# Passes over the experts taken in pairs, with seven places for loaded units and three for split ones in place of five and four

## The chip, the cores and the metric

The kernel runs on one core of one Trainium2 chip. The metric is device time in microseconds (us) of that core. The kernel before has a median of 1789.32 us over 3 runs (1788.54 to 1793.39). The execution that was profiled took 1784.65 us, of which 1782.8 us is the span of its instructions.

## The reference

Two layers of a block with attention, a gated linear recurrence and a feed-forward part, in float32. Only the feed-forward part of the second layer, a mixture of experts on 256 tokens, bears on the change:

```python
def swiglu(h, w1, w3, w2):
    return (jax.nn.silu(h @ w1) * (h @ w3)) @ w2

def moe_ffn(h, router, w1, w3, w2):
    logits = (ht @ router).astype(jnp.float32)
    top_v, top_i = lax.top_k(logits, TOP_K)              # TOP_K = 2 of 8 experts
    wts = jax.nn.softmax(top_v, axis=-1)
    combine = jnp.sum(jax.nn.one_hot(top_i, N_EXPERTS) * wts[..., None], axis=1)
    # for each expert: acc + combine[:, e] * swiglu(ht, w1[e], w3[e], w2[e])
```

The model width is 1024 and the inner width of an expert 2816, so an expert has 3 x 1024 x 2816 weights, 34.6 MB, and all eight 277 MB. The 256 tokens choose two experts each, 512 choices in all, so some experts get many tokens and some few.

## The kernel before

Each expert is one pass. Its weights are cut into 33 units of 1 MB (128 x 2048 floats): for each of 11 chunks of 256 inner columns (FC = 11) two "up" units (w1 and w3, half of the model width each) and one "down" unit (w2). The experts are put in order of their token counts by the kernel itself (`places_ranked`, `columns_ordered`, `experts_ordered`, `ranked` and three times `next_task`, small operations of VectorE (DVE) spread over the first seven chunks of pass 0).

There are two kinds of pass. A full pass (0 to 4) has 128 places for tokens. It computes float32 products from three products of shorter floats (fp32r): ScalarE (ACT) copies a loaded unit `raw` to `w_hi` (`high(s)`), DVE subtracts to get `w_lo` (`low(s)`), and TensorE (PE) does 12 matmuls with each unit (`three`). A narrow pass (5 to 7, the experts with the fewest tokens) has 64 places and reads `raw` directly as float32, without a split, in matmuls that use half of the array's columns each (`up_narrow`, `down_narrow`). Pass 1, `WIDE`, is a full pass with 32 more places.

A pass is a pipeline of steps. In step i PE does the up units of chunk i (`up_chunk`), turns the products of chunk i-1 (`turn_chunk`, transposes) and does the down unit of chunk i-2 (`down_chunk`). ACT takes the silu of the up result (`silu`), DVE multiplies (`product`), and both copy what PE has turned (`columns_turned`, L1463 and L2104 for full, L1460 for narrow). Towards the end of a pass (chunk 7) the tokens of the next pass are picked by matmuls with a selection (`gather`, L2783); in the chunks 3 to 6 of the next pass the output of the last one goes back to its tokens (`scatter`, L2841, 4 pieces, each followed by an addition of DVE, `added`, L2084).

What sets the order:

- SyncE (SP) loads the units in the order in which PE uses them, into a ring of RAW_RING = 5 places. The place of a full unit is free once DVE has split it, that of a narrow unit once PE has used it.
- `w_hi` and `w_lo` have W_RING = 4 places. The split of unit s is written in ACT's and DVE's programs behind PE's use of unit s-4: after unit s-4 is used, ACT copies unit s, then DVE subtracts.
- Each engine runs its program in order and waits on semaphores: a late wait on ACT holds back everything written behind it.
- After the last chunk of pass 7 each engine decides by a branch whether an expert had more tokens than places (it reads `task_i`). For this input it hasn't, and the branch goes over the code of three spare passes to `finish`: ACT copies the last output (`ey_plain`, L1433), PE scatters it, DVE adds, and norm, gate and store follow. RAW_RING units of a spare expert are loaded before that is known, and SP waits for their arrival before it stores.

Of the kernel before, what the change touches and what calls it, by code (L numbers as in the profile page):

```python
# [32 lines left out]
P = 128  # L33
# [19 lines left out]
RING = 3  # L53
# [247 lines left out]
def run_steps(passes):  # L301

    g0, g1 = passes[0] * FC, (passes[-1] + 1) * FC
    for g in range(g0, g1 + 2):
        yield g if g < g1 else None, g - 1 if g0 <= g - 1 < g1 else None, g - 2 if g0 <= g - 2 else None


def pass_units():

    out = []  # L310
    for passes in RUNS:
        for up, _, down in run_steps(passes):
            out += [("up", up, 0), ("up", up, 1)] if up is not None else []
            out += [("down", down)] if down is not None else []
    assert len(out) == PASSES_OF * EXPERT_UNITS
    return out
# [6 lines left out]


def run_last(r):
    return (RUNS[r][-1] + 1) * FC - 1
# [12 lines left out]
NARROW, SLOTS = range(5, EXPERTS), 64  # L339
HALF_GROUPS = P // SLOTS  # L340


def is_narrow(p):

    return p in NARROW
# [11 lines left out]

SPLIT_LIST = [m for m, key in enumerate(UNIT_LIST) if not is_narrow(unit_of_expert(key)[0])]
SPLIT_OF = {m: s for s, m in enumerate(SPLIT_LIST)}

# [6 lines left out]
def split_limit(r):  # L367

    return split_end(r) + (0 if is_narrow(RUNS[r][-1]) else W_RING - 1)
# [8 lines left out]
LATE_SPLIT = SPLIT_OF[UNIT_AT["down", NARROW[0] * FC - 1]]  # L378
# [195 lines left out]
TURN_BANK, SCATTER_BANK = 2, 3  # L574
# [3 lines left out]
def build(nc, ctx, units, x_in, ctx_in, const_in, cols_in, wsm_in, gw2_in, lam_in, rope_in, out):  # L578
# [86 lines left out]
    picked = at("picked", A_GL + 2952, [P, 2, 3, EXPERTS])  # L665
    order, order_parts = at("order", A_AM + 320, [P, EXPERTS, EXPERTS]), at("order_parts", A_GL + 3888, [P, 3, EXPERTS, EXPERTS])
    xt_plain = at("xt_plain", A_ACTT, [P, 2, KT, P])
    selT_plain = at("selT_plain", A_GL + 1280, [P, 2, 2, P])
    eT_plain = at("eT_plain", A_GL + 1792, [P, 2, 256])
    ey_plain = at("ey_plain", A_OD, [P, 512])  # L670
# [13 lines left out]
    raw_more = [at(f"raw_more{i}", (A_V, A_GV)[i], [P, UNIT]) for i in range(2)]  # L684
    w_hi_more, w_lo_more = at("w_hi_more", A_X, [P, UNIT], F32R), at("w_lo_more", A_GG, [P, UNIT], F32R)
# [105 lines left out]
    hi_places = [w_hi[:, (first_w + i) % RING, :] for i in range(RING)] + [w_hi_more[:, :]]  # L791
    lo_places = [w_lo[:, (first_w + i) % RING, :] for i in range(RING)] + [w_lo_more[:, :]]
# [11 lines left out]
    def down_bank(p, h):  # L804

        return 4 + 2 * (p % 2) + h

    def up_bank(g):

        return 0 if g // FC == WIDE else (g + WIDE * FC) % 2  # L810

    def gather_bank(p, n):

        return SCATTER_BANK if p == WIDE + 1 else down_bank(p, n)
# [5 lines left out]
    def select_place(p):  # L820
        return sel if p < EXPERTS else sel_more[p - EXPERTS]
# [14 lines left out]
    def _(sp):  # L836
# [48 lines left out]
        load_more(RING + 1, lambda p: EXPERTS - p)  # L885
        ordered = {0: EXPERTS}
# [36 lines left out]
    def _(pool):  # L923
# [18 lines left out]
        def select_narrow(p):  # L942

            twice = const[:, C_IOTA:C_IOTA + SLOTS].unsqueeze(1).to_broadcast([P, HALF_GROUPS, SLOTS])
            for tt in range(2):
                pool.tensor_scalar(sel[:, tt, :].rearrange("p (j n) -> p j n", j=HALF_GROUPS), twice, route[:, tt, 4, p:p + 1],
                                   route[:, tt, 3, p:p + 1], ALU.is_equal, ALU.mult).then_inc(esem("sel"), 1)
# [11 lines left out]
        for p in range(1, EXPERTS):  # L959

            pool.wait_ge(esem("selT"), p)
# [15 lines left out]
    def _(act):  # L977
# [407 lines left out]
        def half_high(p, n):  # L1385
            act.wait_ge(esem("gathered"), 2 * p + n + 1)
            if is_narrow(p):
                act.activation(xt_plain[:, p % 2, 4 * n:4 * n + 4, 0:SLOTS],
                               psum[:, gather_bank(p, n), 0:4 * SLOTS].rearrange("p (k n) -> p k n", n=SLOTS),
                               ACT.Copy).then_inc(esem("xt_hi"), 1)  # L1390
                return
            act.activation(xt_hi[:, p % 2, 4 * n:4 * n + 4, :],
                           psum[:, gather_bank(p, n), :].rearrange("p (k n) -> p k n", n=P),
                           ACT.Copy).then_inc(esem("xt_hi"), 1)

        def selection_turned(p):
            act.wait_ge(esem("selT"), p + 1)
            if p >= 2:
                act.wait_ge(esem("scattered"), 4 * (p - 1))
            turned_into = selT_plain if is_narrow(p) else selT  # L1400
            act.activation(turned_into[:, p % 2, :, :], psum[:, SCATTER_BANK, 0:256].rearrange("p (t n) -> p t n", t=2),
# [24 lines left out]
        def output(p):  # L1426

            if p:
                act.wait_ge(esem("scattered"), 4 * p)
# [13 lines left out]
        def silu(g):  # L1443
# [5 lines left out]
            if g >= 2:  # L1449
                act.wait_ge(esem("act"), g - 1)  # L1450
            n = P if is_narrow(g // FC) else 256
            act.activation(e_sil[:, g % 2, 0:n], psum[:, up_bank(g), 0:n], ACT.Silu).then_inc(esem("sil"), 1)  # L1452

        def columns_turned(g):

            act.wait_ge(esem("turned"), g + 1)
            if g >= 2:
                wait_used(act, ("down", g - 2))
# [1675 lines left out]
```

## Time and profile before

| | |
|---|---|
| median of 3 runs | 1789.32 us |
| profiled execution | 1784.65 us, span 1782.8 us |
| PE, DVE, ACT busy | 94%, 57%, 44% of the span |
| HBM read | 404.73 MB, mean 229 GB/s over the span |
| full passes 2 to 4 | from 1212.3 us to 1515.3 us |
| narrow passes 5 to 7 | from 1515.3 us to 1766.1 us |
| matmul line L2273 (`three`) | 60% of the chain that ended last |

A time in the profile is from the span's start. The chain of waits follows the work that ended last back through what released it, so in a stretch where its pieces are all PE, PE sets the pace, and where a DMA stands between matmuls, the loads do. The busy share of PE overstates what it does, since a matmul is pipelined: in a full pass one stands for 0.39 us and the next begins 0.227 us after it. So times between starts are used below.

### The profile page before, as it was taken

How to read it: one execution, taken by the hardware profiler on the slowest of the kernel's cores; microseconds unless marked ns; L12 is line 12 of the kernel's file. 1: busy time of each engine (PE TensorE's matmuls, PEld its weight loads, DVE VectorE, ACT ScalarE, POOL GpSimd, SP SyncE). 2: the span in 40 equal slices, each digit the busy share in tenths (PEclk: the TensorE clock that was granted, in tenths of full speed). 3: DMA queues.
4: the chain of work that ended last, by engine and by line, in shares of the span. 5: the costliest groups of instructions: out<-in, count | busy, mean ns of one | idle time of the engine just before them, and what ended most of it. 6: DMA issues, size and time to landing. Idle time of an engine off the chain costs nothing.

```text
span 1782.8 us, 25642 instructions
## 1 busy us (share of the span) xinstructions
PE 1676.5 (94%) x10193; PEld 1294.4 (73%) x10193; DVE 1021.3 (57%) x1415; ACT 792.6 (44%) x1225; POOL 55.0 (3%) x40
## 2 busy tenths in 40 slices
PE   5999987999999999999977999999999999988896
PEld 3877656988888888797767887677788888544443
DVE  3326656677677533733676987657889897100012
ACT  4417544532212222734655766556677776100101
POOL 0000000000000000000000530000000000000000
PEclk9999968999999999999988999999999999999998
DMA  8411053154467532131013986668989998999998
GB/s 335 161 62 72 1 188 144 72 189 174 157 228 262 197 116 95 57 142 63 33 50 142 352 331 227 247 230 328 361 341 356 345 368 313 378 406 421 419 420 363
DMA packets 56831, 407.53 MB, mean 229 GB/s; under 512 B 6322, under 2 KB 6450, under 8 KB 7808
## 3 DMA queue, kind: packets, MB, share of 16 engines
q1 hardware_dynamic: 56128, 404.38, 59.2%
q8 instruction: 84, 1.38, 0.3%
q0 software_dynamic: 288, 0.79, 0.1%
q10 hardware_dynamic: 288, 0.63, 0.1%
q14 instruction: 43, 0.35, 0.1%
HBM read 404.73 MB, written 1.05 MB: 228 GB/s over the span
## 4 chain that ended last, share of the span: by engine, by line
PE 82%; DMA 7%; DVE 6%; ACT 4%; issue 1%; SPq 0%; POOL 0%; ACTq 0%; DVEq 0%
PE psum L2273 60%; DMA raw<-units 5%; PE psum L2887 4%; PE psum L2897 2%; PE psum L2783 2%; DMA raw_more<-units 2%; PE psum L2841 1%; PE psum L2913 1%; PE psum L2925 1%; PE psum L2290 1%; PE psum L2472 1%; PE psum L2299 1%; DVE w_lo L1572 1%; PE psum L2496 1%; ACT xn L1026 1%
## 5 line engine op out<-in xcount | busy, mean ns | idle before, releaser
L1572 DVE TENSOR_TENSOR w_lo<-raw,w_hi 128x1024 fp32r<-128x1024 f32 x130 | 153.0, 1219 | 143.9 <-ACT w_hi L990 143.5
L2273 PE MATMUL psum<-act_hi,w_hi 128*128 128x512 f32 (+1 forms) x608 | 220.3, 362 | 2.8 <-DVE w_lo L1572 2.8
L2273 PE MATMUL psum<-act_hi,w_lo 128*128 128x512 f32 (+1 forms) x608 | 218.1, 359 | 0.0
L2273 PE MATMUL psum<-act_lo,w_hi 128*128 128x512 f32 (+1 forms) x608 | 218.0, 359 | 0.0
L990 ACT ACTIVATE w_hi<-raw 128x1024 fp32r<-128x1024 f32 x130 | 130.4, 1053 | 164.2 <-DMA raw<-units 89.8
L2044 DVE TENSOR_TENSOR w_lo<-raw,w_hi 128x2048 fp32r<-128x2048 f32 x75 | 171.4, 2289 | 45.4 <-ACT w_hi L1378 45.1
L1378 ACT ACTIVATE w_hi<-raw 128x2048 fp32r<-128x2048 f32 x75 | 143.8, 1918 | 73.0 <-PE psum L2273 43.8
L2273 PE MATMUL psum<-w_hi,act_hi 128*128 128x256 f32 (+1 forms) x368 | 131.2, 357 | 4.3 <-DVE act_lo L1651 2.4
L2044 DVE TENSOR_TENSOR w_lo<-raw_more,w_hi 128x2048 fp32r<-128x2048 f32 x49 | 112.1, 2289 | 35.7 <-ACT w_hi L1378 35.4
L2273 PE MATMUL psum<-w_hi,xt_hi 128*128 128x512 f32 x332 | 132.2, 398 | 0.0
L2093 DVE TENSOR_TENSOR e_act<-e_sil,psum 128x256 f32<-128x256 f32 (+1 forms) x88 | 32.2, 366 | 172.6 <-ACT e_sil L1452 172.6
L2273 PE MATMUL psum<-w_lo,xt_hi 128*128 128x512 f32 x332 | 129.9, 391 | 0.0
L2273 PE MATMUL psum<-w_hi,xt_lo 128*128 128x512 f32 x332 | 129.7, 391 | 0.0
L2273 PEld LDWEIGHTS psum<-act_hi,w_hi 128*128 128x128 f32 x608 | 114.9, 189 | 19.6 <-DVE w_lo L1572 3.3
L2273 PEld LDWEIGHTS psum<-act_hi,w_lo 128*128 128x128 f32 x608 | 114.9, 189 | 17.4
L2273 PEld LDWEIGHTS psum<-act_lo,w_hi 128*128 128x128 f32 x608 | 115.0, 189 | 16.3
L2273 PE MATMUL psum<-w_lo,act_hi 128*128 128x256 f32 (+1 forms) x368 | 123.8, 336 | 0.0
L2273 PE MATMUL psum<-w_hi,act_lo 128*128 128x256 f32 (+1 forms) x368 | 123.5, 336 | 0.0
L1452 ACT ACTIVATE e_sil<-psum 128x256 f32<-128x256 f32 (+1 forms) x88 | 29.4, 334 | 198.3 <-PE psum L2887 194.4
L1378 ACT ACTIVATE w_hi<-raw_more 128x2048 fp32r<-128x2048 f32 x49 | 94.0, 1918 | 52.4 <-PE psum L2273 30.7
L1629 DVE SCALAR_TENSOR_TENSOR folded<-raw,c_cols,folded 128x512 f32<-128x512 f32 x140 | 101.5, 750 | 3.3
L2273 PEld LDWEIGHTS psum<-w_hi,act_hi 128*128 128x128 f32 x368 | 70.3, 191 | 27.5 <-issue 12.0
(364 smaller groups left out, 3210.5 us busy)
## 6 DMA issues: line engine op xcount, KB each, us to landing
raw<-units SPq DMA_DIRECT2D x275, 1024.0 KB, 5.1
raw_more<-units SPq DMA_DIRECT2D x107, 1024.0 KB, 6.8
X<-ctx_in SPq DMA_DIRECT2D x1, 1024.0 KB, 8.8
X<-x_in SPq DMA_DIRECT2D x1, 1024.0 KB, 10.8
out<-X SPq DMA_DIRECT2D x2, 512.0 KB, 3.0
const<-const_in ACTq DMA_DIRECT2D x1, 524.0 KB, 7.7
rope<-rope_in POOLq DMA_DIRECT2D x2, 256.0 KB, 4.8
wsm<-wsm_in SPq DMA_DIRECT2D x1, 384.0 KB, 7.8
```

The lines of the kernel that those rows point to most:

```text
L990: act.activation(w_hi[:, w_slot(i), part], raw[:, i % RING, part], ACT.Copy).then_inc(hi_ready, 1)
L1026: act.activation(junk(t), src(t), ACT.Square, accum_out=ssq[:, t:t + 1]).then_inc(done, 1)
L1378: act.activation(w_place(m)[0], raw_place(m), ACT.Copy).then_inc(esem("w_high"), 1)
L1452: act.activation(e_sil[:, g % 2, 0:n], psum[:, up_bank(g), 0:n], ACT.Silu).then_inc(esem("sil"), 1)
L1572: ins = dve.tensor_tensor(w_lo[:, w_slot(i), part], raw[:, i % RING, part], w_hi[:, w_slot(i), part].bitcast(F32), ALU.subtract)
L1629: ins = dve.scalar_tensor_tensor(total, part, share, total, ALU.mult, ALU.add)
L2044: dve.tensor_tensor(lo, raw_place(m), hi.bitcast(F32), ALU.subtract).then_inc(esem("w_ready"), 1)
L2093: dve.tensor_tensor(e_act[:, g % 2, 0:n], e_sil[:, g % 2, 0:n], psum[:, up_bank(g), n:2 * n], ALU.mult).then_inc(esem("act"), 1)
L2273: ins = pe.matmul(dst, lhs(a), rhs(b), start=first and n == 0, stop=last and n == 2)
L2783: ins = pe.matmul(psum[:, gather_bank(p, n), (k % 4) * slots:(k % 4 + 1) * slots], src[:, tt, k * P:(k + 1) * P], select_place(p)[:, tt, 0 ...
L2887: ins = pe.matmul(psum[SLOTS * j:SLOTS * (j + 1), up_bank(g), 0:2 * P].rearrange("p (g n) -> p g n", g=2), xt_plain[:, p % 2, k, 0:SLOTS], ...
L2897: ins = pe.matmul(psum[SLOTS * h:SLOTS * (h + 1), down_bank(p, 0), :], eT_plain[:, g % 2, SLOTS * j:SLOTS * (j + 1)], weight[:, j * D_MODE ...
```

## The change

Passes 2 to 7 are taken in pairs, a full and a narrow one side by side: (2,3), (4,5), (6,7). The narrow passes are now 3, 5 and 7, and a table `PLACE_OF_RANK` gives them the same three experts with the fewest tokens that 5, 6 and 7 had. In a step of a pair PE does the two up units of the full chunk, the two of the narrow one, turns both chunks of the step before, and does the full and then the narrow down unit. The loads follow the same order.

Passes 0 and 1 stay single. There the split of unit s is now written behind the use of unit s-3. In the pairs the split of a unit is written in its own step. The two places that `w_hi_more` and `w_lo_more` had become places for loaded units: RAW_RING = 7, W_RING = 3. A narrow pass has its own small buffers (`e_sil_plain`, `e_act_plain`, `sel_plain`), so that it can go beside a full one. The gather for the next pair is cut into pieces in the chunks 7 to 10, the scatters of the pair before stand in the chunks 2 to 9. The ranking in pass 0 has eight more tiny writes (`place_wanted`), two more comparisons and one more operation in each `next_task`. At the end two passes, 6 and 7, are still to be scattered.

```diff
+PLACE_OF_RANK = (0, 1, 2, 5, 3, 6, 4, 7)
-RAW_RING, W_RING = 5, 4
+RAW_RING, W_RING = 7, 3
+NARROW, SLOTS = (3, 5, 7), 64
+FIRST_PAIR = 2
+def run_steps(r):
+    rows = []
+    for p in RUNS[r]:
+        if not is_narrow(p):
+            beside = (p + 1,) if is_narrow(p + 1) else ()
+            rows += [tuple(q * FC + c for q in (p,) + beside) for c in range(FC)]
+    for i in range(len(rows) + 2):
+        yield tuple(rows[j] if 0 <= j < len(rows) else () for j in (i, i - 1, i - 2))
-def split_behind(r, key):
-    s = SPLIT_OF[UNIT_AT[key]] + W_RING
-    return [s] if s < split_limit(r) and s != LATE_SPLIT else []
+def splits_at(r, key):
+    s = SPLIT_OF[UNIT_AT[key]]
+    if r == 0 and s >= SINGLE_SPLITS:
+        return [s]
+    return [s + W_RING] if s + W_RING < (split_limit(r) if r else SINGLE_SPLITS) else []
+def gather_pieces(r, p, c):
+    if r or p == 0 or is_narrow(p) or not 0 <= c - GATHER_STEP < 4:
+        return []
+    a = p + 1 if p == WIDE else p + 2
+    pieces = [[(a, 0)], [(a, 1)], [(a, 2), (a + 1, 0)], [(a + 1, 1), (a + 1, 2)]][c - GATHER_STEP]
+    return [piece for piece in pieces if piece[0] <= EXPERTS]
...
@@ ACT, run(r): a step of a pair; DVE's has low, added, product in the same places
+                for g in full:
+                    for s in splits_at(r, ("up", g, 0)):
+                        high(s)
...
+                    for s in splits_at(r, ("up", g, 1)):
+                        high(s)
+                if is_paired(r, i):
...
+                    for g in turned_into_rows(r, i):
+                        columns_turned(g)
+                    for q, piece in gathered_into_rows(r, i):
+                        half_high(q, piece) if piece < 2 else selection_turned(q)
+                for g in full:
+                    if g // FC != WIDE:
+                        silu(g)
+                if is_paired(r, i):
+                    for g in downs[:1]:
+                        for s in splits_at(r, ("down", g)):
+                            high(s)
+                    for g in ups[1:]:
+                        silu(g)
+                    continue
...
@@ DVE
-            output(RUNS[r][-1])
+            for q in last_passes(r):
+                output(q)
...
         def finish(p):
+            for q in last_passes(0)[:-1] if p < EXPERTS else ():
+                for n in range(4):
+                    added(q, n, n)
...
@@ PE
-            for up, turned, down in run_steps(RUNS[r]):
...
+            for ups, turned, downs in run_steps(r):
+                for g in ups:
+                    up_chunk(g)
+                for g in turned:
+                    turn_chunk(g)
+                for g in downs:
+                    down_chunk(g)
...
         def finish(p):
-            for n in range(4):
-                scatter(p, n, n)
+            for q in last_passes(0) if p < EXPERTS else (p,):
+                for n in range(4):
+                    scatter(q, n, n)
```

ACT's program in a full pass of before, one step and the beginning of the next (`w_hi` is a split's copy, `e_sil` the silu of a full chunk, `eT_hi` its turned columns; in brackets the semaphores that an instruction waits for):

```order
L1378 ACTIVATE w_hi<-raw_more_150 128x2048 [waits more_arrived3,e_w_used]
L1378 ACTIVATE w_hi_more<-raw_more_151 128x2048 [waits more_arrived4,e_w_used]
L1378 ACTIVATE w_hi<-raw 128x2048 [waits more_arrived0,e_w_used]
L1452 ACTIVATE e_sil<-psum 128x256 [waits e_act,e_w_used]
L1463 ACTIVATE eT_hi<-psum 128x256 [waits e_w_used,e_turned]
```

And in a step of a pair (`e_sil_plain` and `eT_plain` are the narrow chunk's):

```order
L1511 ACTIVATE w_hi<-raw 128x2048 [waits more_arrived2,e_w_used]
L1511 ACTIVATE w_hi<-raw_more_154 128x2048 [waits more_arrived3,e_w_used]
L1599 ACTIVATE eT_hi<-psum 128x256 [waits e_w_used,e_turned]
L1597 ACTIVATE eT_plain<-psum 128x128 [waits e_w_used,e_turned]
L1588 ACTIVATE e_sil<-psum 128x256 [waits e_act,e_w_used]
L1511 ACTIVATE w_hi<-raw_more_157 128x2048 [waits more_arrived6,e_w_used]
L1586 ACTIVATE e_sil_plain<-psum 128x128 [waits e_act,e_w_used]
```

The three splits of a step stood in a row, ahead of the silu. Now the third, that of the step's down unit, stands behind the silu of the full chunk, and the next step's first split behind the silu of the narrow chunk.

DVE's program where pass 7 ends and the branch is taken, before (`e_act` is the product of silu and gate, `ey_lo` a part of a full pass's output, `y_moe` the sum over experts):

```order
L2093 TENSOR_TENSOR e_act<-e_sil,psum 128x128 [waits e_turned,e_sil] x3
L826 TENSOR_LOAD task_i [waits tasks,emptied1,emptied0]
L826 ISA x2
L2232 COMPARE_AND_BRANCH
```

And now:

```order
L2191 TENSOR_TENSOR w_lo<-raw_more_154,w_hi 128x2048 [waits e_w_high]
L2219 TENSOR_TENSOR ey_lo<-psum,ey_hi 128x512 [waits e_ey_hi] x2
L954 TENSOR_LOAD task_i [waits tasks,emptied1,emptied0]
L954 ISA x2
L2409 COMPARE_AND_BRANCH
```

The last output of full pass 6 (`ey_lo`) now stands ahead of DVE's branch, and it waits for ACT's `ey_hi`, which stands behind ACT's own branch.

## Rows read from the trace of the kernel before

**Rows 1.** Stages: length; PE, PEld, DVE, ACT, POOL busy; clock, DMA share, GB/s.

```profile
976.40:1072.60 96.20, 96.20 (x461) 79.61 (x461) 88.08 (x107) 68.77 (x60) 40.50 (x18) 0.99 0.86 321
...
1212.30:1318.90 106.60, 106.60 (x493) 83.03 (x490) 85.92 (x63) 71.93 (x62) 1.88 (x2) 1.00 0.88 345
...
1417.10:1515.30 98.20, 98.20 (x462) 81.24 (x463) 83.17 (x62) 67.35 (x58) 1.88 (x2) 1.00 0.90 343
1515.30:1766.10 250.80, 226.90 (x1506) 117.01 (x1505) 23.87 (x51) 25.80 (x83) 1.56 (x2) 0.99 1.00 410
```

**Rows 2.** Chain of waits in full pass 3: start us, us, what.

```profile
1307.70 8.21 PE psum L2273 x36
...
1316.13 8.21 PE psum L2273 x36
```

**Rows 3.** Chain of waits in narrow pass 6, first and second up unit.

```profile
1636.04 1.95 PE psum L2887 x16
...
1643.48 1.95 PE psum L2887 x16
```

**Rows 4.** PE in pass 7 with its units already loaded (start, us, engine, operation).

```profile
1744.88 0.33 PE L2925 MATMUL psum<-const,e_act 128*128 128x128 f32 x1
1745.13 1.94 PE L2897 MATMUL psum<-raw,eT_plain 128*64 128x512 f32 x8
1746.90 3.62 PE L2887 MATMUL psum<-raw,xt_plain 128*64 128x256 f32 x32
1750.46 0.33 PE L2925 MATMUL psum<-const,e_act 128*128 128x128 f32 x1
```

**Rows 5.** A unit's boundary on PE, and ACT around it, in pass 0.

```profile
1004.51 0.36 ACT L1452 ACTIVATE e_sil<-psum 128x256 f32<-128x256 f32 x1
1004.77 0.37 ACT L1463 ACTIVATE eT_hi<-psum 128x256 fp32r<-128x256 f32 x1
...
1008.38 1.92 ACT L1378 ACTIVATE w_hi<-raw_more 128x2048 fp32r<-128x2048 f32 x1 [0.80 <-PE psum L2273]
...
1008.18 0.39 PE L2273 MATMUL psum<-w_hi_more,xt_hi 128*128 128x512 f32 x1
```

**Rows 6.** Chain of waits where a split was late, at the first narrow pass.

```profile
1522.15 1.92 ACT w_hi L1378
...
1526.54 3.01 PE psum L2273 x12
```

**Rows 7.** Chain of waits: scatters of passes 1, 2 and 5, gathers of 4 and 7.

```profile
1249.17 1.71 PE psum L2841 x4
...
1352.55 0.45 PE psum L2841 x2
...
1640.52 1.05 PE psum L2841 x2
...
1388.01 3.52 PE psum L2783 x32
...
1655.44 3.69 PE psum L2783 x32
```

**Rows 8.** DVE in pass 0: a tiny write, and one of the three next_task.

```profile
987.66 0.06 DVE L2161 MEMSET score<- 128x1 f32 x1
...
1019.25 0.15 DVE L2194 TENSOR_REDUCE top<-rank 128x1 f32<-128x8 f32 x1
...
1021.57 2.29 DVE L2044 TENSOR_TENSOR w_lo<-raw,w_hi 128x2048 fp32r<-128x2048 f32 x1
```

**Rows 9.** Chain of waits behind ACT's branch, then ACT and DVE behind it.

```profile
1762.37 5.22 issue
...
1767.59 1.28 ACT L1520 ACT_TABLE_LOAD   x1 [5.74 <-issue]
...
1771.16 1.41 DVE L2084 SCALAR_TENSOR_TENSOR y_moe<-psum,route,y_moe 128x512 f32<-128x512 f32 x2 [12.86 <-PE psum L2841]
```

**Rows 10.** Thirty microseconds of pass 2, columns as in rows 1.

```profile
1235.00:1265.00 30.00, 30.00 (x130) 23.01 (x129) 26.01 (x19) 20.80 (x18) 0.00 (x0) 1.00 1.01 423
```

More of the change, by code:

```diff
@@ L355, in full_chunks_before, with own_row, same_before, parity @@
     return full_before(g // FC) * FC + g % FC
+def own_row(p):
+    return (p - full_before(p) if is_narrow(p) else full_before(p)) % 2
+def same_before(p, n=2):
+    rows = [q for q in range(PASSES_OF) if is_narrow(q) == is_narrow(p)]
+    at = rows.index(p) - n
+    return rows[at] if at >= 0 else None
+def parity(g):
+    p, c = divmod(g, FC)
+    n = p - full_before(p) if is_narrow(p) else full_before(p)
+    return (n * FC + c) % 2
+def two_before(g):
+    rows = [h for h in CHUNKS if is_narrow(h // FC) == is_narrow(g // FC)]
+    at = rows.index(g) - 2
+    return rows[at] if at >= 0 else None
+def up_bank(g):
+    p = g // FC
+    if p == WIDE:
+        return 0
+    if FIRST_PAIR <= p < EXPERTS:
+        return int(is_narrow(p))
+    return (g + WIDE * FC) % 2
+def up_bank_before(g):
+    rows = [h for h in CHUNKS[:CHUNK_AT[g]] if up_bank(h) == up_bank(g)]
+    return rows[-1] if rows else None
 SPLIT_LIST = [m for m, key in enumerate(UNIT_LIST) if not is_narrow(unit_of_expert(key)[0])]
 SPLIT_OF = {m: s for s, m in enumerate(SPLIT_LIST)}
+SINGLE_SPLITS = sum(m < UNIT_AT["up", FIRST_PAIR * FC, 0] for m in SPLIT_LIST)
 def split_end(r):
@@ new lines, in run @@
+                for g in full:
+                    if g // FC != WIDE:
+                        silu(g)
+                if is_paired(r, i):
+                    for g in downs[:1]:
+                        for s in splits_at(r, ("down", g)):
+                            high(s)
+                    for g in ups[1:]:
+                        silu(g)
+                    continue
+                for g in turned_into_rows(r, i):
+                    columns_turned(g)
+                for g in downs[:1]:
+                    for s in splits_at(r, ("down", g)):
+                        high(s)
@@ new lines, in run @@
+                for q, piece in gathered_into_rows(r, i):
+                    half_high(q, piece) if piece < 2 else selection_turned(q)
+                for g in full:
+                    p, c = divmod(g, FC)
+                    if c == GATHER_STEP and (p == 0 or r and p + 1 < PASSES_OF):
+                        columns_high(p + 1)
+                    if p == WIDE - 1 and c == GATHER_STEP + 1:
+                        wide_columns()
+                    if p == WIDE - 1 and c == GATHER_STEP + 2:
+                        wide_selection_turned()
@@ L2854, in up_chunk @@
             p, c = divmod(g, FC)
-            if g >= 2:
-                pe.wait_ge(esem("act"), g if p == WIDE and c else g - 1)
+            if up_bank_before(g) is not None:
+                pe.wait_ge(esem("act"), CHUNK_AT[up_bank_before(g)] + 1)
             if p == WIDE + 1 and c == 0:
@@ L2994, in finish @@
         def finish(p):
-            for n in range(4):
-                scatter(p, n, n)
+            for q in last_passes(0) if p < EXPERTS else (p,):
+                for n in range(4):
+                    scatter(q, n, n)
         def extra(k):
```

430 lines of the change are left out of this document (244 added, 186 removed).

## The prediction

> **What bounds the kernel now.** I read the stages first. In the full passes PE is busy all the time and the 16 DMA engines have room (348 GB/s or less, share 0.88 to 0.90); in the three narrow passes, 250.8 us long, the DMA share is 1.00 at 410 GB/s, while DVE and ACT are busy for about 10% [rows 1]. The chains of waits say the same. In a full pass they hold nothing but matmuls, and a step of one chunk (36 matmuls and two transposes) takes 1316.13 - 1307.70 = 8.43 us [rows 2]. In a narrow pass the second up unit of a step starts only as its load lands, 1643.48 - 1636.04 = 7.44 us from step to step [rows 3], 2.48 us for each of three units. Its own PE work is less: with the units loaded already, a step takes 1750.46 - 1744.88 = 5.58 us [rows 4], of which 0.14 us is a wait between turn and down unit (0.25 us, where the transpose by itself needs some 0.11); 5.44 us is left. So one kind of pass is bound by PE and the other by the loads, and side by side they would share both.
>
> **The bound that pairs could reach.** The loads of a pair are 66 units x 2.48 = 164 us. PE's work is 11 x (8.43 + 5.44) = 152.6, plus gathers and scatters: 3.8 (full gather with its transposes) + 3.9 (narrow gather) + 4 x 0.45 + 4 x 1.05 [rows 7], 166 us in all. Before, a full and a narrow pass take 98.2 + 250.8/3 = 181.8 us [rows 1]. Some 15 us for each of three pairs is there to be had, if nothing else waits.
>
> **What a step of a pair waits for.** Take T as the start of a step's first up unit on PE. The full up units end at T + 5.46 (24 matmuls at 0.227). ACT's program has the split of the step's down unit behind the silu of this very chunk. ACT starts 0.20 us after PE has gone on (1008.38 - 1008.18), and the next copy can start 0.26 us after a silu (1004.77 - 1004.51) [rows 5]. From the start of a split's copy to the first matmul that uses it takes 1526.54 - 1522.15 = 4.39 us [rows 6]. So the down unit is ready at T + 5.46 + 0.20 + 0.26 + 4.39 = T + 10.31. PE has the narrow up units (3.56) and the transposes (0.22 + 0.13) in between and is at the down unit at T + 9.37. It waits 0.9 us in every step. The down units take 2.73 + 1.77, so a step is 14.8 us; with a first matmul of 0.1 us more in some I take 14.85. The next step's first split starts at T + 9.02 + 0.12 + 0.25, behind the narrow silu, and is ready at T + 13.8, before it is wanted: it hides, with 1 us to spare. The loads need 6 x 2.48 = 14.9 us a step and average less than PE with its gathers and scatters; the ring of seven carries the difference, since the place of the second narrow up unit, for instance, is read at T + 9, more than 10 us before what goes into it is wanted.
>
> **Sum of the stage,** from the start of pass 2 (1212.3) to PE's last down unit (1766.1), 553.8 us before. After: 31 whole steps x 14.85 = 460.4; two steps that still hold the wide pass's down units (10.31 + 2.95 + 1.0 each) 28.6; the two steps behind the last up unit 9.9 (turn, down 2.73 + 1.77, a split that is ready at 5.4, 2.73 + 1.77 again); scatters of pass 1 4 x 1.71 = 6.8, of two full passes 8 x 0.45 = 3.7 and two narrow ones 8 x 1.05 = 8.4; gathers 3 x 3.8 + 2 x 3.9 = 19.2. That is 537.0, and the narrow gather of pass 3, 3.9, now lies in pass 1, which is PE's too: 540.9, **-12.9 us**. The bounds of the step: 13.9 if the split were never late (it can't be shorter), which gives the stage about 25 us less as far as the loads let it; above, 15.3, at which a pair gains nothing ((181.8 - 13.7)/11), and what the slow rivals below give.
>
> **Pass 0 with three split places.** A split is started when unit s-3 has been used and is wanted two units, 5.45 us, later. Its 0.20 + 4.39 leave 0.9 us to spare, where four places left 3.6. DVE's work for a chunk is 83.17/11 = 7.56 of 8.43 us [rows 1], so it has 0.87 us left over in each. Over the first seven chunks it also ranks: three next_task of 1021.57 - 1019.25 = 2.32 us (11 operations, 0.21 each) [rows 8] and 19 more operations, about 4.0 us, 11.0 in all. The change adds 8 writes at 0.09 (0.06 busy), two comparisons and three operations at 0.21, 1.8 us. Free time is 7 x 0.87 = 6.1. So DVE is late by up to 12.8 - 6.1 = 6.7 and PE waits for what is over 0.9: 5.8 us. Before it was 4.9 less 3.6, 1.3 at most. I take **+5.0**. Bounds: 0, if it is hidden as most of it is now, and 8. In pass 1 the wide pass's own matmuls stand between the units and lengthen a step, while DVE has hardly more to do, so three places are enough: 0.
>
> **The tail.** ACT goes over the branch in 5.22 us and starts its table load 5.74 us after its last copy [rows 9]; that is late even now, the scatters wait for it. In the new program ACT's last work of the passes is the split of the last down unit, 7 us before PE ends, so branch and table load (1.4) end at about PE's end, 2.7 us earlier than before in relation to it. Then come two `ey_hi` (1.0) and `ey_plain`, and DVE's second `ey_lo`, 2.1 us behind PE's end. DVE's branch is behind that one. I take 5.7 us for it, as ACT's; it shows nowhere in the trace, since DVE had 12.86 us of idle time for it [rows 9], so it is between 0 and that. DVE then has four additions of pass 6, 0.7 each, and after them the same finish as now, 1782.8 - 1771.16 = 11.6, less a wait of 0.3. Sum: 2.1 + 5.7 + 2.8 + 11.3 = 21.9 us behind PE's last down unit, where it was 16.7. **+5.2 us** (0 to +12). The seven loads of a spare expert take 7 x 2.48 = 17.4 us, issued up to PE's end: they land within the tail and cost nothing.
>
> That the branch takes longer than its own instruction is in the Trainium skill too: "Runtime: NRT & Kernel Launch", section "Instruction fetch mechanics", says that a taken branch out of the fetched window has to fetch its target by DMA first. ACT's 5.22 us agree. "Advanced Engine Details and Errata", section "Control Flow Timing", gives about 108 ns for a compare-and-branch; by that figure for DVE's branch the tail would be 5.6 us shorter than my sum and cost nothing.
>
> **Sum:** -12.9 + 5.0 + 5.2 = -2.7 us, on the profiled execution 1784.65 - 2.7 = 1782.0. The median of before lies 4.7 us above that execution, so I forecast 1786.6, in round figures 1787: no change that a measurement can tell (0.3%, 5.4 us).
>
> **Rivals.**
>
> *The split is not late (fast).* If the step is 13.9 us, because the silu's place costs less than I think, PE and loads are even, and the stage ends some 24 us earlier: 1763. Against it: the chain from the up units' end has four terms, each from a row, and there is no slack in it beyond the 3.9 us of narrow work. 15%.
>
> *The ends cost less (fast).* DVE's branch is short or hidden, and part of the ranking's lateness too: -8 to -10, 1778. For it: DVE's branch is unseen, and DVE was never waited for in the tail. 15%.
>
> *The loads become the bound (slow).* In the full passes 1 MB costs more DMA time: share 0.90 at 343 GB/s is 381 GB/s for a busy engine [rows 1], 2.75 us a unit, 16.5 a step. Then a pair takes 66 x 2.75 = 181.6 against PE's 11 x 14.85 + 13.7 = 177: +5 a pair, and more, since steps without gathers wait for loads and the others for PE, which the ring can only level over a step or so: 11 x 16.5 + 6 x 1.5 = 190. With that +40 us in all, 1825 at the far end, 1810 as its middle. It decides from 2.68 us a unit on. Against it: over 30 us of pass 2, with DVE busy for 26 and ACT for 21 of them, the core loaded 423 GB/s [rows 10], 2.48 us a unit. 10%.
>
> The Trainium skill speaks for this one: "DMA: Bandwidth & Descriptors", section "Specifications", gives about 358 GB/s as what HBM gives one core. At that a pair would be 66 x 2.93 = 193 us and the change slower by some 50 us. The 410 GB/s of the narrow passes [rows 1] and the 423 of pass 2 are against it.
>
> *More waits than one in a step (slow).* ACT and DVE have 14.8 us of step and run each other's programs late, say at the first steps of a pair, where outputs, gathered halves and selections stand before the silu: 0.3 us a step more, +10: 1797. 12%.
>
> **Chances.** My sum 48%, the rivals 15, 15, 10 and 12. Around my sum I allow 8 us either way, of which 35% lies below -5.4, 50% within and 15% above. Faster: 0.17 + 0.15 + 0.13 = 0.45. Same: 0.24 + 0.02 + 0.02 = 0.28. Slower: 0.27. The range of eight in ten goes from 1763 to 1806; the likeliest case's own is 1779 to 1795.
>
> **What would show it.** In the profile after: steps of about 14.8 us in a pair without gather, in each a wait of PE for DVE's `w_lo` of 0.9 us ahead of the down unit and none ahead of the up units; hardly any wait for a DMA in the pairs, at 390 GB/s; the start of pass 2 near 1221; PE's last down unit near 1758; and 22 us from there to the end, with 5 to 6 us of idle DVE behind the second `ey_lo`. I am wrong if the chain shows DMAs between the matmuls of the pairs, if PE doesn't wait for `w_lo` there, or if pass 0 is as long as before.

## The result, and the profile after

The changed kernel takes 1803.36 us (median of 4 runs, 1801.58 to 1805.38), the kernel before 1789.68 us (4 runs). The ratio is 1.0076, with a 95% interval of 1.0056 to 1.0097: **slower by 0.76%**, 13.7 us, where I had forecast no change (1787). The profiled execution has a span of 1800.0 us, where my sum gives 1780.1.

Stages of the changed kernel, columns as in [rows 1]: passes 2 to 7 in pairs up to ACT's branch, and a stretch of 8.5 us in pass 2.

```profile
1224.90:1771.50 546.60, 521.65 (x2837) 346.30 (x2837) 276.94 (x231) 225.90 (x261) 5.35 (x6) 0.99 0.96 376
1258.30:1266.80 8.50, 8.50 (x26) 6.50 (x28) 3.56 (x4) 0.75 (x4) 0.00 (x0) 0.66 0.64 252
```

In the pairs PE is busy for 95% and the DMA engines are near their limit, 376 GB/s on average: the loads of the narrow passes [rows 1] are spread over all six passes, as meant. But PE is idle for 25 us. What it waits for there (releaser; us in total, times, longest us):

```profile
PE psum L2451 <- DVE w_lo L2191: 24.9, 34, 4.9
```

The kernel before has 0.6 us of this in one place, and 15.3 us of waits for DMAs in its narrow passes, of which the pairs of the changed kernel have none. One step of a pair in its chain of waits (start us, us, what), without scatter or gather:

```profile
1426.86 5.72 PE psum L2451 x24
...
1432.88 1.91 ACT w_hi L1511
...
1434.81 2.30 DVE w_lo L2191
...
1437.25 2.98 PE psum L2451 x12
1440.24 1.87 PE psum L3088 x8
1442.10 0.43 PE psum L2451
```

The step takes 1442.10 - 1426.86 = 15.24 us. It is the chain that I had worked out: up units, silu, copy, difference, down unit. PE waits 0.61 us in it. In the kernel before, a full and a narrow pass (4 and 6) took 98.2 and 81.9 us one behind the other, 180.1 us from start to start; the pair (4, 5) takes 181.1 us: nothing is gained.

The third step of pass 2 has a hole that I had not seen. Its chain, and ACT at the same place (start, us, operation, idle time before and its releaser):

```profile
1253.90 1.91 ACT w_hi L1511
...
1258.27 8.46 PE psum L2451 x24
```

```profile
1253.41 0.60 ACT L1551 ACTIVATE ey_wide<-psum 128x512 f32<-128x512 f32 x1 [4.79 <-PE psum L3160]
```

`wide_output` (L1551) waits for pass 1's last down unit and stands ahead of the next step's two splits in ACT's program. PE has to wait 4.93 us, and its 24 matmuls then take 8.46 us in place of 5.49: the first 13 start some 0.43 us apart, at the lower of the clock's two levels (1.2 of 2.4 GHz; granted 0.66 on average over this stretch). That is 7.9 us in one place.

Pass 0 in the chain of waits, its start, one `next_task` inside it, the first up units of chunk 9, and those of chunk 10:

```profile
978.78 6.46 PE psum L2451 x24
...
1023.22 0.08 DVE top L2368
...
1025.67 0.39 DVE w_lo L2191
...
1050.34 5.48 PE psum L2451 x24
...
1062.28 7.21 PE psum L2451 x24
```

The same places in the kernel before:

```profile
976.37 11.97 PE psum L2273 x48
...
1043.40 5.48 PE psum L2273 x24
...
1055.33 5.60 PE psum L2273 x24
```

From 984 to 1038 us the changed kernel's chain is almost all DVE. The stretch up to 1050.34 takes 71.56 us, before 67.03. The 7.21 us behind it were 5.60 before, at a granted clock of 0.76 instead of 1.00.

The tail: ACT's branch, the first `ey_lo`, DVE's branch behind the second, the first addition (chain), and PE's last down unit (PE's own list).

```profile
1771.46 5.00 issue
...
1778.47 0.57 DVE ey_lo L2219
...
1780.06 5.35 issue
...
1785.48 0.76 DVE y_moe L2231
```

```profile
1778.25 1.94 PE L3088 MATMUL psum<-raw_more,eT_plain 128*64 128x512 f32 x8
```

From PE's last down unit (1780.1) to the end are 19.9 us; before they were 16.7.

### The profile page after: what moved, and what is told of

Read it like the earlier page. It is cut to its first block, busy times and chain, and to the rows that moved or that the text cites. A ratio compares the mean times of both kernels' runs of the same rounds, so it can differ in the third digit from the quotient of the medians.

```text
span 1800.0 us, 25641 instructions
## 1 busy us (share of the span) xinstructions
PE 1689.3 (94%) x10193; PEld 1291.8 (72%) x10193; DVE 1024.7 (57%) x1428; ACT 782.2 (43%) x1225; POOL 48.0 (3%) x40
## 4 chain that ended last, share of the span: by engine, by line
PE 76%; DVE 12%; ACT 7%; issue 3%; DMA 1%; SPq 0%; POOL 0%; ACTq 0%; DVEq 0%
PE psum L2451 57%; DVE w_lo L2191 6%; ACT w_hi L1511 4%; PE psum L3088 3%; PE psum L2961 2%; PE psum L3032 1%; DMA raw<-units 1%; PE psum L3104 1%; PE psum L2650 1%; PE psum L2468 1%; PE psum L2477 1%; DVE w_lo L1719 1%; PE psum L2674 1%; ACT xn L1159 1%; PE psum L3160 1%
## 5 line engine op out<-in xcount | busy, mean ns | idle before, releaser
L2191 DVE TENSOR_TENSOR w_lo<-raw_more,w_hi 128x2048 fp32r<-128x2048 f32 x94 | 214.0, 2291 | 83.9 <-ACT w_hi L1511 83.7
L1511 ACT ACTIVATE w_hi<-raw_more 128x2048 fp32r<-128x2048 f32 x94 | 178.0, 1909 | 42.6 <-PE psum L2451 19.5
L2191 DVE TENSOR_TENSOR w_lo<-raw,w_hi 128x2048 fp32r<-128x2048 f32 x71 | 161.6, 2290 | 61.3 <-ACT w_hi L1511 61.1
L2451 PE MATMUL psum<-w_hi,xt_hi 128*128 128x512 f32 x440 | 178.5, 406 | 8.6 <-DVE w_lo L2191 8.6
L2451 PE MATMUL psum<-w_lo,xt_hi 128*128 128x512 f32 x440 | 174.0, 395 | 0.0
L2451 PE MATMUL psum<-w_hi,xt_lo 128*128 128x512 f32 x440 | 173.5, 394 | 0.0
L1588 ACT ACTIVATE e_sil<-psum 128x256 f32<-128x256 f32 x55 | 20.9, 380 | 232.9 <-PE psum L2451 232.9
L2243 DVE TENSOR_TENSOR e_act<-e_sil,psum 128x256 f32<-128x256 f32 x55 | 23.0, 417 | 171.6 <-ACT e_sil L1588 171.6
L2451 PEld LDWEIGHTS psum<-w_hi,xt_hi 128*128 128x128 f32 x440 | 84.0, 191 | 37.7 <-issue 19.0
L2451 PE MATMUL psum<-w_hi,eT_hi 128*128 128x512 f32 x220 | 90.7, 412 | 20.2 <-DVE w_lo L2191 20.2
```

The source lines that it names most:

```text
L1511: act.activation(w_place(m)[0], raw_place(m), ACT.Copy).then_inc(esem("w_high"), 1)
L1588: act.activation(e_sil[:, parity(g), :], psum[:, up_bank(g), 0:256], ACT.Silu).then_inc(esem("sil"), 1)
L2191: dve.tensor_tensor(lo, raw_place(m), hi.bitcast(F32), ALU.subtract).then_inc(esem("w_ready"), 1)
L2243: dve.tensor_tensor(e_act[:, parity(g), :], e_sil[:, parity(g), :], psum[:, up_bank(g), 256:512], ALU.mult).then_inc(esem("act"), 1)
L2451: ins = pe.matmul(dst, lhs(a), rhs(b), start=first and n == 0, stop=last and n == 2)
```

## Experiments

Kernels that have the same program up to pass 0 start it anywhere from 975 to 985 us in their profiled executions, whatever is edited later. So stages are compared from their own start. All times are against runs of the kernel before on the same chip; the columns are A, start of pass 0 to start of pass 2, and B, from there to the end of the span, both from the profiled execution.

| kernel | ratio to before, 95% interval | A | B |
|---|---|---|---|
| before | 1 | 235.9 | 570.5 |
| changed | 1.0076 (1.0056 to 1.0097) | 246.1 | 575.1 |
| e1_wide_output | 1.0041 (1.0027 to 1.0055) | 246.3 | 568.2 |
| e2_split_first | 0.9943 (0.9924 to 0.9962) | 246.2 | 549.4 |
| e3_narrow_first | 0.9961 (0.9944 to 0.9978) | 246.1 | 552.9 |
| e4_rank_later | 1.0070 (1.0053 to 1.0087) | 243.2 | 575.2 |
| e5_tail | 1.0059 (1.0037 to 1.0081) | 246.0 | 569.8 |
| g1_pairs_five_four | 1.0148 (1.0119 to 1.0176) | 243.1 | 595.9 |
| g2_single_seven_three | 1.0011 (0.9996 to 1.0026) | 238.6 | 567.2 |
| f2_wide_and_split | 0.9898 (0.9868 to 0.9928) | 246.0 | 541.3 |
| f4_split_and_narrow_first | 0.9909 (0.9883 to 0.9936) | 246.2 | 544.8 |
| f5_before_turns | 0.9890 (0.9868 to 0.9912) | 246.2 | 541.7 |
| f8_before_turns_tail | 0.9863 (0.9837 to 0.9889) | 246.0 | 535.7 |
| f9_split_tail | 0.9856 (0.9835 to 0.9877) | 246.2 | 536.0 |

In all kernels with pairs A holds a narrow gather of 4.0 us that lay in B before. The last two have other rings and are told at the end. The profiled execution of g1_pairs_five_four took 1825.81 us, 9.8 us more than the median of its six, so its B overstates the difference.

**The hole in pass 2.**

```diff
-                    if p == WIDE + 1 and c == 2:
-                        wide_output()
                     for s in splits_at(r, ("up", g, 0)):
                         high(s)
 ...
                 if is_paired(r, i):
+                    if full and divmod(full[0], FC) == (WIDE + 1, 2):
+                        wide_output()
```

> The changed kernel, with ACT's copy of pass 1's output (wide_output) moved behind the two high splits of its step instead of ahead of them. Theory A (the hole in pass 2's third step is one of the three things that cost the change its gain): the wait of PE there, 4.93 us, and the half clock behind it, about 3 us, go: 8 us less than the changed kernel, 1795. Rival: the same time, 1803, since the next step's work on ACT and DVE is then late by as much, or since the chunk's copies of the output hold PE's first down unit instead.

B falls by 6.9 us, where I had expected 8, and the ratio by 0.35%. PE's waits for `w_lo` over the whole layer are now as follows (28.9 us in 39 waits in the changed kernel; the longest that is left, 1.2 us, lies in pass 0, in the pairs none is over 0.7), and ACT does `ey_wide` with 1.22 us of waiting that nobody sees:

```profile
PE psum L2451 <- DVE w_lo L2191: 24.0, 38, 1.2
```

```profile
1252.02 0.60 ACT L1551 ACTIVATE ey_wide<-psum 128x512 f32<-128x512 f32 x1 [1.22 <-PE psum L3160]
```

The granted clock at the same place is 1.00. Theory A holds: the wait and the half clock behind it go together.

**The late split.**

```diff
+                if is_paired(r, i):
+                    for g in downs[:1]:
+                        for s in splits_at(r, ("down", g)):
+                            high(s)                        # low(s) on DVE
                 for g in full:
                     if g // FC != WIDE:
                         silu(g)                            # product(g) on DVE
                 if is_paired(r, i):
-                    for g in downs[:1]:
-                        for s in splits_at(r, ("down", g)):
-                            high(s)
                     for g in ups[1:]:
                         silu(g)
```

> The changed kernel, with the split of a pair's first down unit (ACT's copy and DVE's difference) ahead of the silu and the product of the full chunk instead of behind them. My step of 14.85 us held 0.9 us of waiting for that split; the trace has 0.61 us in most of 33 steps, 24.9 us of PE waiting for DVE's w_lo in all (5 of them behind wide_output). Theory A: this wait goes and nothing takes its place: about 18 us less than the changed kernel, 1785, steps of 14.6 us where no scatter lies. Rival B: the silu now starts some 1 us later and DVE's product behind 1.8 us of low work, so that the transpose of the narrow chunk or the next step's first split is late in its place: 0 to -5 us, 1798 to 1803. If A holds fully, the rest of the loss lies in PE's own work (a step of 14.6 against the 13.9 that I took as the floor).

B falls by 25.7 us, more than theory A's 18. The waits over the whole layer (in the pairs two are left, 5.2 us, 4.9 of them in the hole of pass 2), and a step, which is PE alone:

```profile
PE psum L2453 <- DVE w_lo L2192: 8.9, 6, 4.9
```

```profile
1419.15 5.71 PE psum L2453 x24
1424.86 3.60 PE psum L3080 x32
1428.46 0.37 PE psum L3121 x2
...
1428.94 2.77 PE psum L2453 x12
1431.71 1.87 PE psum L3090 x8
1433.58 5.71 PE psum L2453 x24
```

The step is 14.43 us, 0.81 less than 15.24; 31 times that are 25.1 us, nearly all of B's gain. So the late split cost 0.81 us: 0.61 of idle time, and 0.2 that appears as longer work beside it (the down unit 2.98 and not 2.77). The expectation fell short because it priced the restart at nothing. The silu and product that now stand behind the split make nothing late.

**Narrow down unit first.** The same wait is removed from the other side: PE reaches the full down unit later.

```diff
-        yield tuple(rows[j] if 0 <= j < len(rows) else () for j in (i, i - 1, i - 2))
+        ups, turned, downs = (rows[j] if 0 <= j < len(rows) else () for j in (i, i - 1, i - 2))
+        yield ups, turned, downs[::-1]
 ...
-                    act.wait_ge(esem("out_half"), p + 1)
+                    act.wait_ge(esem("out_half"), p + 1 + is_narrow(p + 1))
```

> The changed kernel, with a pair's narrow down unit ahead of its full down unit on PE (it needs no split). With the split still behind the silu, PE would be at the full down unit at T + 9.75 + 1.87 = T + 11.6, the split ready at T + 10.4. Theory A (the wait for the late split is what the steps lose, 0.61 us and some 0.15 for the restart): no wait in the steps, 14.4 us as in the run with the split first, 1779. Theory B (each change between full and narrow matmuls costs 0.1 to 0.25 us, which is why a step without any wait takes 14.43 and not 13.95): the last narrow work now stands beside the other narrow work, two changes fewer: the first up units take 5.49 in place of 5.71, a step 14.2, 1772. Rival: the longer path to the end of the full down unit makes the next split late, 1790 or more.

```profile
1427.50 3.60 PE psum L3079 x32
...
1431.59 1.87 PE psum L3089 x8
1433.45 8.39 PE psum L2452 x36
1441.84 3.60 PE psum L3079 x32
```

A step is 14.34 us and without a wait: theory A. Theory B's 14.2 isn't reached: the up units, which now stand behind a full unit, are shorter, but the narrow down unit, now behind the transposes, begins later (a table below has the pieces). B is 3.5 us longer than in e2_split_first although the step is shorter. The full output is now the last one, and PE's last down unit is followed by 21.8 us in place of 20.3. The other 2 us lie in the pairs: their third step, the one with the hole, takes 21.91 us in place of 20.09, and steps with a scatter of pass 1 16.08 in place of 15.91. Why the hole is longer wasn't tested.

**Both edits that paid, and the narrow unit first besides.**

> Both edits that each brought time: wide_output behind the two high splits, and the down unit's split ahead of the silu. If they take away separate waits their gains add up: 0.35% + 1.3% less than the changed kernel, ratio to the kernel before 0.9908, 1772 to 1773. Rival: the hole in pass 2's third step stays, since a load lands late there in the run with the split first (DMA ahead of w_hi in its chain): 0.9943 as with the split alone.

> The version with both edits, and the narrow down unit first on PE besides. By theory B (changes of kind cost) 0.22 us a step less than both edits alone, 33 steps: 7 us, 1765. By theory A alone, that only the waits counted, the same as both edits, 1772. A third: steps of 14.2 us with six units of 2.48 = 14.9 us to load now wait for DMAs, and the stage is bound by loads: 1768 or more, with waits for raw<-units in the pairs.

The first two add up, 0.9898 where I had expected 0.9908. The rival falls: in the pairs PE waits for `w_lo` for 0.6 us in all, the hole is gone too. The pair (4, 5) now takes 172.1 us in place of 181.1. With the narrow unit first there is no further gain (0.9909, intervals overlap), for the reasons just seen; the expectation of 1765 by theory B failed.

**All narrow work of a step in one piece.**

```diff
                 for g in ups:
                     up_chunk(g)
+                for g in downs[:-1]:
+                    down_chunk(g)
                 for g in turned:
                     turn_chunk(g)
-                for g in downs:
+                for g in downs[-1:]:
                     down_chunk(g)
```

(With narrow first and `wide_output` moved, as above. The split of the full down unit stays behind the silu.)

> The changed kernel with wide_output moved, and on PE the narrow down unit of a step straight behind the narrow up units, ahead of both transposes; the full down unit comes behind them. Steps of the run with narrow first took 14.34 us without any wait, of which my old sum (13.87, from passes that run alone) leaves 0.47 unexplained. Theory B: 0.23 of it come at the change from a narrow down to a full unit and 0.15 at that from narrow up units to the transposes; with all narrow work in one piece only one change is left, 0.15 to 0.2 us less a step, 14.15; ratio 0.9961 - 0.0035 (wide_output) - 0.003 = 0.9895, 1769. Rival: the cost isn't tied to the number of changes, and the step is 14.34 again: 0.9926, 1775.

A step of the chain without scatter or gather:

```profile
1318.83 3.60 PE psum L3079 x32
1322.43 1.72 PE psum L3089 x8
1324.15 0.37 PE psum L3120 x2
1324.52 0.11 PE psum L3117
...
1332.83 3.60 PE psum L3079 x32
```

1332.83 - 1318.83 = 14.00 us. The pieces of a step, each from its own first matmul to that of the next piece in PE's list (the pieces of a chain go from end to end, and the ends are modelled):

| step | full up | narrow up | transposes | full down | narrow down | sum |
|---|---|---|---|---|---|---|
| passes that run alone, before | 5.44 | 3.56 | 0.25 | 2.85 | 1.77 | 13.87 |
| split first (as in the changed kernel's order) | 5.71 | 3.60 | 0.30 | 2.95 | 1.87 | 14.43 |
| narrow down unit ahead of the full one | 5.53 | 3.61 | 0.48 | 2.86 | 1.86 | 14.34 |
| all narrow work in one piece | 5.53 | 3.50 | 0.30 | 2.85 | 1.82 | 14.00 |

So theory B fits the work: counting the transposes as full work, a step with one change from narrow to full takes 14.00 us, with two 14.34 or 14.43. That the order costs time is shown; that it goes by the number of changes is read from three orders only.

But little of this reaches the time. 0.9890 is near the 0.9895 that I had expected, and within the intervals it is no better than 0.9898 with the split first. PE's last down unit is followed by 22.5 us in place of 20.0, the first two steps of pass 2 wait for a split (14.34 us each for 13.92), and from 1416 us on DMAs stand in the chain, here one whose place came free with PE's narrow down unit (SP issues it, it lands 10.95 us later). Under it is the whole stage:

```profile
1443.79 1.74 PE psum L3089 x8
...
1445.70 10.95 DMA raw_more<-units
...
1456.73 1.92 ACT w_hi L1512
```

```profile
1224.00:1740.00 516.00, 510.87 (x2858) 350.14 (x2857) 278.27 (x231) 231.31 (x260) 4.36 (x4) 1.00 0.99 401
```

The DMA share is 0.99. In the four steps of the pair (4, 5) that have 14.00 us of work and a scatter of 0.45, one takes 15.55 us and three 14.90: there the six loads of a step (6 x 2.48 = 14.9) are the bound.

**The tail.**

```diff
-            for q in last_passes(r):          # end of DVE's run(r)
-                output(q)
         def finish(p):
+            for q in last_passes(0) if p < EXPERTS else (p,):
+                output(q)
```

(The same in `extra`, for the spare passes.)

> The changed kernel, with DVE's ey_lo of the last full pass moved behind its branch over the spare passes. Step of my tail tested alone: DVE's branch, 5.35 us between the second ey_lo and the first addition, begins only at PE's end and is the new term of the tail. Moved ahead, it should lie beside the last down units: 5 us less than the changed kernel, 1798, and PE's end to the end of the span 14.5 us instead of 19.9. Rival: the branch starts no earlier or takes as long beside other work, and PE's or ACT's own branch is the one that counts: 0, 1803.

```profile
1785.84 0.68 PE psum L3034 x2
...
1786.54 0.03 DVE y_moe L2231
```

1800.4 - 1785.84 = 14.6 us from PE's last down unit to the end, in place of 19.9: DVE's branch is out of the chain. B falls by 5.3, as expected. The ratio is 0.17% less, with intervals that overlap; in the two kernels below the same edit brings 0.27% and 0.42%, again with intervals that overlap, and B falls by 6.0 and 5.3.

**Put together.**

> The kernel with wide_output moved and all narrow work of a step in one piece, and DVE's ey_lo behind the branch besides. If the three kinds of loss (late split, changes of kind, branch in the tail) are separate, the gains add: 0.9895 - 0.003 = 0.9865, 1764. Rival: the branch's gain is absent when PE's last unit is the full one (ey_hi then starts later anyway): as without it.

> wide_output moved, the down unit's split ahead of the silu, and DVE's ey_lo behind the branch: 0.9898 as without the last of the three, less 5 us for the branch: 0.987, 1765. Rival: 0.9898, 1770, if another engine's branch takes its place.

0.9863 and 0.9856. In B the gains of `wide_output`, split and branch alone add up to 37.9 us (6.9 + 25.7 + 5.3), and f9_split_tail has 39.1: these three losses are separate. That the changes of kind are a fourth isn't shown in the time: the kernel that saves them (0.9863) is not faster than the one that doesn't (0.9856). f9_split_tail, 1761.18 us, has the lowest median: 1.4% under the kernel before. Its pairs:

```profile
1224.00:1740.00 516.00, 515.39 (x2850) 344.82 (x2849) 279.24 (x231) 230.05 (x259) 5.03 (x6) 1.00 0.99 400
```

PE is idle for 0.6 of 516 us there and the DMA share is 0.99. That is the balance that the change was to reach.

**Pass 0: three places or the ranking?** One kernel moves the last part of the ranking to pass 1, another is the kernel before with the new rings only, a third the changed kernel with the old rings.

```diff
-                    if p == 0 and c == 3:
+                    if p == WIDE and c == 0:
                         ranked()
-                    if p == 0 and 4 <= c < 4 + EXTRA:
-                        next_task(c - 4)
+                    if p == WIDE and 1 <= c < 1 + EXTRA:
+                        next_task(c - 1)
```

```diff
-RAW_RING, W_RING = 5, 4        # the kernel before, passes one by one
+RAW_RING, W_RING = 7, 3
```

```diff
-RAW_RING, W_RING = 7, 3        # the changed kernel, passes in pairs
+RAW_RING, W_RING = 5, 4
```

(In both with the buffers that go with the rings.)

> The changed kernel, with DVE's last part of the ranking and the three next_task moved from pass 0's fourth to seventh chunk to pass 1's first to fourth. Theory A (pass 0 is longer because DVE's extra ranking work no longer fits beside three split places): pass 0 gets shorter by the work moved, 3 x 2.45 us and the ranked part of about 1.5 us, as far as it was waited for: 5 us, 1798. Rival: pass 1 gets longer by as much, 1803, since DVE has no more room there.

> The kernel before (passes one by one, in the old order), with seven places for loaded units and three for split ones, and nothing else of the change. My step for pass 0: three split places leave 0.9 us to spare in place of 3.6, and cost most of +5.0 us there; so 1789.7 + 4 = 1794. In the narrow passes the loads are the bound, and two places more let them run ahead at their start: up to -2 us. Rival: three places cost nothing (1789, or 1787 with the gain of the seven), and pass 0's 6 us come from the added ranking operations alone.

> The changed kernel's pairs with the old rings, five places for loaded units and four for split ones. If the three split places are what makes pass 0 longer, pass 0 is back at its old length (5 us less); the single passes with seven and three cost only 0.1% in the other run, so I rather expect 1 to 2 us there. In the pairs each split may start a unit earlier, so the wait for the late split goes as far as ACT's program lets it: it doesn't, since the silu stands ahead of it either way: 0.6 us a step stays (theory A: position in ACT's program); rival: it goes (theory: number of places). With five places for loads a narrow unit's place comes free late and PE waits for DMAs in the pairs: steps of over 16 us in pairs, 1830; rival: five are enough, 1800.

Start of pass 0 and of its chunk 9, first with the ranking moved, then in the old order with seven and three places:

```profile
979.31 6.50 PE psum L2451 x24
...
1047.95 5.48 PE psum L2451 x24
```

```profile
980.25 6.34 PE psum L2271 x24
...
1049.87 5.48 PE psum L2271 x24
```

| | pass 0 up to chunk 9 |
|---|---|
| before | 67.03 |
| old order, seven and three places | 69.62 |
| changed | 71.56 |
| changed, ranking moved | 68.64 |
| changed, five and four places | 68.60 |

So of 4.5 us the three places make 2.6 and what else the change does in pass 0, the added operations of the ranking, the other 1.9. Moving the ranking gives back 2.9, where I had expected 5, and A keeps all of it (243.2), so pass 1 had room for it: the rival for pass 1 falls. The time shows 0.06% less, which is within the interval. The old order with the new rings is at 1.0011 (0.9996 to 1.0026), where I had expected 1794 us, 0.25% more. In its profiled execution A is 2.7 us longer and B 3.3 us shorter than before: the seven places give back what the three cost. With five and four places in the changed kernel pass 0 up to chunk 9 is 3.0 us shorter, nearly the same price of the three places once more, and 1.6 us are left for the ranking. But the pairs are slower, by 0.72% in the ratios and 20.8 us in B: the ring of five is too short for pairs. The chain there:

```profile
1449.80 7.53 DMA raw_more<-units
...
1461.79 3.00 PE psum L2452 x12
```

```profile
1228.00:1780.00 552.00, 512.74 (x2766) 338.47 (x2766) 271.61 (x225) 227.16 (x252) 7.73 (x6) 0.99 0.93 363
```

The loads are waited for at a DMA share of 0.93: it is not their rate, it is that they are issued late. Whether four split places would take the late split away can't be told here, since a DMA stands ahead of the splits. Steps of over 16 us are there (16.4 to 16.9 us where a scatter of 0.45 lies in them, 15.70 in the changed kernel), but the time that I gave (1830) was too high, measured 1816.

## Why the prediction was wrong

The mechanism of each part was right but for one, a wait in the pairs that I had left out; the sum of the pairs was too small, most of all by their work. The measured 1803 lies within the range of eight in ten (1763 to 1806), but I had filled its slow end with loads and waits, not with longer work.

- **What bounds the kernel; the loads as a rival: right.** No matmul in the pairs waits for a DMA, at 376 GB/s on average, and at 401 in the kernel of f5. The Trainium skill's 358 GB/s for a core ("DMA: Bandwidth & Descriptors", "Specifications") is passed by those 401 over 516 us. My argument that a loaded engine keeps 2.48 us a unit held: the steps of f5_before_turns that wait for loads take 14.90 us for six units.
- **The step of 14.85 us: this is what failed, by a mis-sized term.** My sum had 13.87 us of work and 0.98 of waiting and small change; measured are 14.43 and 0.81. I had added up durations of a full pass and a narrow pass that run alone [rows 2, 4]. Side by side the pieces are longer: by the table above, up units by 0.27, the two down units by 0.10 each, transposes by 0.05, narrow up units by 0.04, 0.56 us in all. f5_before_turns shows that most of it (0.43) goes with the order of full and narrow units, since the same pieces in another order take 14.00. It stood in the trace of before, in pass 1's last steps, where transposes stand behind the wide pass's narrow matmuls (0.37 in place of 0.22) and full up units behind its narrow down unit (5.68 in place of 5.47):

```profile
1207.80 0.37 PE psum L2925 x2
...
1212.37 5.68 PE psum L2273 x24
```

I had read neither. 31 x 0.56 = 17.4 us, less 31 x 0.17 = 5.3 for the wait: +12.1.
- **The late split: right,** place and reason. The run with the split first shows what it costs, 25 us, three times my whole error margin. I had priced it and left it at that; it was the largest single thing in the change.
- **No other wait in the pairs: wrong.** `wide_output` stands ahead of a split, 7.9 us with the clock's fall. As a rival I had listed outputs ahead of the silu at 0.3 us a step; it was one place, and ahead of the splits. To find it I should have followed ACT's program at the seam between pass 1 and the pairs, where it waits for the last thing that PE does. The stage: 537.0 + 12.1 + 7.9 = 557.0; measured 555.2. The sum is too high there, since in the 12 steps with a scatter of a full pass the up units take 5.49 and not 5.71.
- **Pass 0: +5.0 forecast,** +4.5 up to chunk 9, and 1.6 more at the lower clock in chunk 10, 6.2 from start to start. Of the 4.5 us, 2.6 to 3.0 come from the places and 1.6 to 1.9 from the ranking. The fall of the clock I had not forecast. It is there in every kernel with pairs, with the old rings too (the up units of chunk 10 take 6.95 to 7.23 us), and in neither kernel without (5.60); why stays open.
- **The tail: +5.2 forecast, +3.2 measured.** DVE's branch takes 5.35 us (I took 5.7) and begins behind the second `ey_lo` as described; that one ends 0.5 us before PE's last down unit and not 2.1 us after it, since ACT is through with its branch and table load at 1777.7 us, 2.4 before PE's end and not at it. The run with `ey_lo` behind the branch confirms the branch as the term. The Trainium skill's 108 ns for a compare-and-branch ("Advanced Engine Details and Errata", "Control Flow Timing") isn't what a branch over this much code takes: 5.00 us on ACT and 5.35 on DVE. The Trainium skill also says that a target out of the fetched window must be fetched first ("Runtime: NRT & Kernel Launch", "Instruction fetch mechanics"). The two times agree with that, but no run here shows the fetch itself.
- **The rest:** the span of 1800.0 is 19.9 over my sum: 18.2 in the stage, 1.2 in pass 0, 2.4 from a later start of pass 0, which isn't the change's, less 2.0 in the tail.

## What to carry to other kernels

Work that is bound by matmuls and work that is bound by loads can be put side by side, and it paid here (1.4%), but only once every chain through the other engines ended before PE came to it; a chain that is 0.6 us late in each step cost all the gain. Write what PE waits for ahead of what it doesn't, in each engine's program, and look at the seams between two kinds of pass first. Durations of two kinds of work that run alone don't add up to a step of both: find a place in the trace where the two already stand next to each other.

## What I had not expected of the hardware

- The same five pieces of a step take 14.43, 14.34 or 14.00 us on PE by their order alone, and 13.87 added up from passes that hold one kind only. The full up units take 5.71 us behind a narrow unit (64 columns of the array) and 5.53 behind a full one, from start to start. What in the array or its weight loads does this wasn't tested.
- A wait of 0.61 us for another engine costs PE 0.81, as the work behind it is longer too.
- After 4.93 us without work PE went on at half its clock for 5.7 us; after the waits of up to 0.7 us in the pairs of e1_wide_output it did not (granted clock 1.00 there).
